# Gates, branches and the first half chunk of merge in one stage; exchanged banks and an earlier Gelu in the gather; unread products in pauses of TensorE

## The reference

```python
x = first_block(...)       # layer 0: retention; layer 1: forgetting attention; each h @ w_in, mixer, @ w_out
# second block
proj = rms_norm(x, mix_norm_w) @ w_in          # stick-breaking q k v, delta-rule q k v z b a, gate_sb, gate_gdn
o_sb  = stick_breaking_attention(q, k, v)
o_gdn = rms_norm(gated_delta_rule(...), gdn_out_norm_w) * silu(z)
merged = sigmoid(gate_sb) * (o_sb @ w_branch_sb) + sigmoid(gate_gdn) * (o_gdn @ w_branch_gdn)
x = x + merged @ w_out
h2 = rms_norm(x, ffn_norm_w)
# PEER: per token 8 heads x 16 experts out of 16384
s1, s2 = h2 @ w_q against keys1, keys2;  expert = top 16 of the sums of the top 16 of each
x = x + sum_e softmax(score)_e * gelu(h2 . u[e]) * v[e]
```

## Time and profile before

| | |
|---|---|
| median of 3 runs | 3151.41 us (3150.56 to 3151.66) |
| the profiled execution's own time | 3151.18 us |
| its span, first to last instruction | 3149.4 us |
| PE busy | 2786.7 us (88%) |
| DVE busy | 1850.0 us (59%) |
| ACT busy | 904.6 us (29%) |
| POOL busy | 738.3 us (23%) |
| mean granted TensorE clock | 0.954 |
| gather's queue (software_dynamic) | 536.90 MB, 41.0% of 16 engines' span |

### The profile page before, as it was taken

One profiled execution on the slowest core, in us unless ns is written; L12 is line 12 of the kernel. 1 busy time (PEld: TensorE's weight loads), 2 busy tenths in 40 slices (PEclk: granted clock), 3 DMA queues, 4 the chain that ended last, 5 costly groups with the idle time before them and its releaser, 6 DMA issues. The chain is left out here.

```text
span 3149.4 us, 29124 instructions
## 1 busy us (share of the span) xinstructions
PE 2786.7 (88%) x10720; PEld 1841.8 (58%) x10720; DVE 1850.0 (59%) x3613; ACT 904.6 (29%) x1686; POOL 738.3 (23%) x724
## 2 busy tenths in 40 slices
PE   7999999999899999999999989778777777777877
PEld 6887587766677677889877873333333333333333
DVE  7761634343543657455534478777677777777554
ACT  3123313433355746422422332111111111111111
POOL 0000210000110523253000124333333333333432
PEclk8999999999999999999999999998989989998999
DMA  7574655521545454644523379999999999999997
GB/s 277 206 275 164 184 180 169 187 81 54 174 160 187 134 189 161 220 132 125 200 80 127 107 269 420 422 421 422 422 422 422 422 422 422 422 422 422 422 422 309
DMA packets 190006, 840.75 MB, mean 267 GB/s; under 512 B 17060, under 2 KB 19364, under 8 KB 123431
## 3 DMA queue, kind: packets, MB, share of 16 engines
q0 software_dynamic: 73728, 536.90, 41.0%
q1 hardware_dynamic: 116136, 301.98, 28.1%
HBM read 828.34 MB, written 144.71 MB: 309 GB/s over the span
## 5 line engine op out<-in xcount | busy, mean ns | idle before, releaser
L230 DVE TENSOR_TENSOR weights_low<-weights_raw,weights_high 128x2048 fp32r<-128x2048 f32 x108 | 250.5, 2320 | 415.2 <-ACT weights_high L225 405.6
L225 ACT CAST weights_high<-weights_raw 128x2048 fp32r<-128x2048 f32 x108 | 206.0, 1907 | 612.8 <-PE proj_banks L288 594.5
L288 PE MATMUL proj_banks<-h_low,weights_high 128*128 128x512 f32 x896 | 357.3, 399 | 14.3 <-PEq L161 6.2
L288 PE MATMUL proj_banks<-h_high,weights_high 128*128 128x512 f32 x896 | 351.8, 393 | 0.0
L288 PE MATMUL proj_banks<-h_high,weights_low 128*128 128x512 f32 x896 | 351.8, 393 | 0.0
L3128 ACT ACTIVATE coef<-dots 128x4 f32<-128x4 f32 x126 | 25.9, 205 | 794.0 <-DVE dots L3006 794.0
L3109 ACT ACTIVATE sig<-shape_consts,coef 128x128 f32<-128x128 f32 x512 | 163.9, 390 | 251.1 <-DVE coef L3025 251.1
L288 PEld LDWEIGHTS proj_banks<-h_low,weights_high 128*128 128x128 f32 x896 | 170.1, 190 | 53.7 <-issue 17.3
L2906 PE MATMUL work_banks<-rows_over_split,sig 128*128 128x512 f32 x256 | 144.0, 703 | 54.6 <-ACT sig L3109 54.6
L288 PEld LDWEIGHTS proj_banks<-h_high,weights_low 128*128 128x128 f32 x896 | 170.1, 190 | 36.6 <-issue 1.9
L288 PEld LDWEIGHTS proj_banks<-h_high,weights_high 128*128 128x128 f32 x896 | 170.0, 190 | 36.0
(11 more groups left out here) (524 smaller groups left out, 5651.2 us busy)
## 6 DMA issues: line engine op xcount, KB each, us to landing
joined_rows<-in_peer_u_dram SPq DMA_DIRECT2D x64, 1024.0 KB, 7.2
joined_rows<-in_peer_v_dram SPq DMA_DIRECT2D x64, 1024.0 KB, 7.2
weights_raw<-in_w_in_dram SPq DMA_DIRECT2D x36, 1024.0 KB, 5.0
weights_raw<-in_ret_w_in_dram SPq DMA_DIRECT2D x24, 1024.0 KB, 5.3
ret_gate<-in_mod_w_dram SPq DMA_DIRECT2D x20, 1024.0 KB, 12.3
weights_raw<-in_fox_w_in_dram SPq DMA_DIRECT2D x16, 1024.0 KB, 5.4
weights_raw<-in_ret_w_out_dram SPq DMA_DIRECT2D x8, 1024.0 KB, 5.3
weights_raw<-in_peer_w_q_dram SPq DMA_DIRECT2D x8, 1024.0 KB, 5.4
```

The costliest lines, as they stand in the source:

```text
L225: nc.scalar.copy(whi[h][:, :, :], raw[h][:, :, :]).then_inc(high_ready[h], 1)
L230: nc.vector.tensor_tensor(wlo[h][:, :, :], raw[h][:, :, :], whi[h][:, :, :].bitcast(F32), ALU.subtract).then_inc(w_split[h], 1)
L288: last = nc.tensor.matmul(out_tile, lhs, rhs, start=(start and j == 0), stop=(stop and j == 2))
```

## The change

**The stage.** `gates` becomes `gated_branches`. Its block goes on after the four gate chunks with the two chunks of w_branch_sb, the two of w_branch_gdn and the first half of w_out's first chunk. The ends of three blocks become one. The inputs of the later products are split inside the earlier chunks: o_sb during gate chunks 1 and 2, the delta rule's output during the sb chunks, the merged tiles as each is added. They go into the places of tiles that are no longer used. `output_norm` gets the split input (`begun`) and starts at the second half of its first chunk. On ACT the second copy of each turned pair moves behind the sigmoids.

**The gather.** Rows and sums change banks: for even t they lie in `pb`, for odd t in `pa`. DVE waits for the last chunk's first two tiles only, ACT issues a Gelu on one column at once, then puts the first group's Gelu and diagonals between its four score copies. DVE waits for all score copies after the first group.

**The unread products.** `idle_products` issues fp32 products of the identity with constants into a bank that nobody reads after them. In program order there are 17: one ahead of each of the last three transpose groups of the retention's attention and two behind them, two at the end of each of the three `output_norm`, six at the end of the forgetting attention.

The diff, cut to its core:

```diff
@@ -337,6 +337,11 @@
+    def idle_products(to, n):
+
+        for _ in range(n):
+            nc.tensor.matmul(to, ident, cst[:, 0:S], start=True, stop=True)
+
@@ -388,7 +393,7 @@
-            inp = InputSplit(tag, src, input_parts(st, tag + "in_", tiles), tiles)
+            inp = begun or InputSplit(tag, src, input_parts(st, tag + "in_", tiles), tiles)
...
-                    load(sp, w_src, 1, g0 + 1)
+                    if begun is None:
+                        load(sp, w_src, 1, g0 + 1)
...
                     for c in range(n):
-                        half_product(c, 0, range(TT))
+                        if c or begun is None:
+                            half_product(c, 0, range(TT))
...
                     for t in range(TT):
                         turn(t)
+                    pe.wait_ge(tile_free[0], stored(1))
+                    idle_products(pb[:, 0, :], 2)
...
@@ -1087,7 +1100,9 @@
                         for n in range(RET_HEADS * TT - LAG, RET_HEADS * TT):
+                            idle_products(pb[:, 0, :], 1)
                             transposes(n)
+                        idle_products(pb[:, 0, :], 2)
@@ -1563,6 +1578,7 @@
                             values(m)
+                        idle_products(pb[:, 0, :], 6)
@@ -2566,11 +2582,16 @@
-    def gates(parts, qkv, sig, osb, ogt, o_away, z_away, then):
+    def gated_branches(parts, qkv, sig, osb, ogt, o_away, z_away, dead, kept):
...
+        SB, GDN, OUT = n, n + D // CW, n + 2 * D // CW
...
+        for tiles in dead:
+            tiles.close()
+        over_left, over_out, over_z = (sbuf(kept, "branch_in_over_" + k, [P, KT, S], F32R) for k in ("left", "out", "z"))
...
+            sb_in = InputSplit("sb_branch_", osb, (over_left, over_z), KT)
+            gdn_in = InputSplit("gdn_branch_", ogt, (over_out, over_osb), KT)
+            out_in = InputSplit("merge_", sig, (over_left, over_z), KT)
...
-                    for c in range(1, n):
-                        load(sp, columns(a["w_in_2"][0], 7 * D + 2 * H), c, g0 + c, join=False)
+                    for c in range(1, OUT + 2):
+                        load(sp, sources[min(c, OUT)], c, g0 + c, join=False)
...
                 @block.tensor
...
+                    for c in range(SB, OUT):
+                        inp = sb_in if c < GDN else gdn_in
+                        for h in range(2):
+                            project_half(pe, c, h, inp.parts, ready=inp.ready)
+                    project_half(pe, OUT, 0, out_in.parts, feature_major=False, ready=out_in.ready)
                 @block.vector
...
+                        if c == 1:
+                            sb_in.low(range(KH))
+                        elif c == 2:
+                            sb_in.low(range(KH, KT))
+                    dve.wait_ge(odd_read, TT)
+                    for c in range(SB, GDN):
+                        split_second(low, c)
+                        split_next(low, c)
+                        gdn_in.low(range((c - SB) * KH, (c - SB + 1) * KH))
+                        for t in range(4):
+                            m = 4 * (c - SB) + t
+                            dve.wait_ge(tile_full[t], g0 + c + 2)
+                            nc.vector.tensor_tensor(sig[:, m, :], sig[:, m, :], pb[:, t, :], ALU.mult
+                                                    ).then_inc(tile_free[t], 1)
+                    for c in range(GDN, OUT):
...
+                            if t:
+                                out_in.low(range(m - 1, m))
+                        out_in.low(range(4 * (c - GDN) + 3, 4 * (c - GDN) + 4))
+                    split_second(low, OUT)
                 @block.scalar
...
-                        for t in range(2 * c - 4, 2 * c - 2) if c >= 2 else ():
...
+                        if c >= 2:
+                            keep_odd(2 * c - 4)
                         for t in range(4):
                             act.wait_ge(tile_full[t], g0 + c + 2)
...
+                        if c >= 2:
+                            keep_odd(2 * c - 3)
+                        if c == 1:
+                            act.wait_ge(og_ready, TT)
+                            act.wait_ge(o_back, 16)
+                            sb_in.high(range(KH))
+                        elif c == 2:
+                            sb_in.high(range(KH, KT))
...
+                    for c in range(GDN, OUT):
+                        split_second(high, c)
+                        split_next(high, c)
+                        for m in range(4 * (c - GDN), 4 * (c - GDN) + 4):
+                            act.wait_ge(added, m + 1)
+                            out_in.high(range(m, m + 1))
+                    split_second(high, OUT)
-            stage_end(n)
+            stage_end(OUT)
...
@@ -2873,10 +2910,10 @@
-                return (pb[:, 0:2, :] if t % 2 else pa[:, 2:4, :]).rearrange("p b n -> p (b n)")
+                return (pa[:, 2:4, :] if t % 2 else pb[:, 0:2, :]).rearrange("p b n -> p (b n)")
...
-                return pb[:, 2 + half, :] if t % 2 else pa[:, half, :]
+                return pa[:, half, :] if t % 2 else pb[:, 2 + half, :]
@@ -2996,7 +3033,8 @@
-                    dve.wait_ge(sc_ready, 4 * n)
+                    for b in range(2):
+                        dve.wait_ge(tile_free[b], state["g"] + n + 1)
@@ -3049,6 +3087,8 @@
                                 weights_of(t, g)
+                                if g == 0:
+                                    dve.wait_ge(sc_ready, 4 * n)
@@ -3098,16 +3138,25 @@
+                    nc.scalar.activation(coef[:, 0, 0:1], eps[:, 0:1], ACT.Gelu).then_inc(gelu_table, 1)
...
+                    for t in range(TT):
+                        if t == TT - 2:
+                            act.wait_ge(dot_done, PRE + GE)
+                            act.wait_ge(gelu_table, 1)
+                            nc.scalar.activation(coef[:, 0, :], dots[:, 0, :], ACT.Gelu).then_inc(gelu_done, 1)
+                        act.wait_ge(s_full, 4 * (n - 1) + t + 1)
+                        if t == TT - 1:
+                            act.wait_ge(coef_ready, 1)
+                            diagonals(0)
+                        nc.scalar.copy(sc[:, t, 4 * n - 4:4 * n, :],
+                                       pa[:, t, :].rearrange("p (f c) -> p f c", c=P)).then_inc(sc_ready, 1)
```

115 lines of the change are left out of this document (49 added, 66 removed).

## The result

| | before | after |
|---|---|---|
| median | 3151.41 us (5 runs, 3150.56 to 3153.49) | 3122.00 us (5 runs, 3120.72 to 3123.78) |
| the profiled execution's own time | 3151.18 us | 3121.36 us |
| its span | 3149.4 us | 3119.5 us |
| PE busy | 2786.7 us (88%) | 2795.8 us (90%) |
| DVE busy | 1850.0 us (59%) | 1852.3 us (59%) |

The change saves 29.4 us; the ratio is 0.9907, with a 95% interval from 0.9896 to 0.9918. The forecast was 3123.6 in a range from 3119.0 to 3132.5.

What follows compares the result with a forecast made beforehand. The prediction took DMA to bound the gather and PE everything ahead of it. Its terms, 7.6 + 16.8 + 1.2 + 2.2 = 27.8 us, taken from 3151.18 with the median 0.23 higher, gave 3123.6 us, range 3119 to 3132.5.

Steps and rivals of the forecast that it cites:

- What bounds the kernel: Whole kernel: DMA bounds the gather at 422 GB/s, PE bounds ahead of it; each us PE saves there shortens the end.
- Unread products ahead of the merge: Retention's attention, first output_norm, forgetting attention, second output_norm: gains of 1.9, 1.7, 2.7 and 1.3, sum 7.6 us.
- These lie between the two. I take them as held: Pauses left at first output_norm and forgetting attention, some 1.6 and 1.7 us, between 1.27 and 2.39: no low clock assumed.
- the 0.4 at the second `output_norm`: Second output_norm: unread products end at 884.8, DVE at 884.47; this later end is taken off the 1.7 us gain.
- behind 2.39 and more the slow stretch comes: Reading of PE's pauses: slow records follow pauses of 2.39 us and more, at once or 1 to 1.5 us later.
- the clock falls all the same: Rival: unread products fill only part of each pause; two pauses failing gives 3128.0 (0.13), all five 3134.1 (0.07).
- The joined stage: Gates to w_out: four pauses go, worth 1.4, 7.1, 4.3 and 4.0 us, sum 16.8, if the splits fit beside PE.
- The thinnest cover: Joined stage: x and a weight split take 10.1 us against PE's half chunk of 10.9, leaving 0.8 us; no wait assumed.
- the term for ACT's copies: Inside the gates: PE's 1.27 us wait for the sigmoids goes with ACT's second copy behind them, worth 1.4 us.
- Merge to the gather's stage: Behind the merge: two unread products save the clock's 1.6 us less 0.4 of a later end, 1.2.
- The opening: Gather's opening: earlier rows and first PE product close the DMA hole from 1875 to 1895, worth 2.2 us (1.6 to 2.7).
- The other rivals: Joined stage waits, 3129.5 (0.12); PE bounds the gather, 3159 (0.03); the end doesn't follow PE, 3148 (0.03).

Runs made afterwards that it cites:

- e4: The kernel before with the 17 unread products alone, without joined stage or new gather: 3145.23 us, 6.8 below before.
- e2: The changed kernel with the gather's part undone (old banks, all four score copies ahead of the first Gelu): 3126.43 us.
- e1: The changed kernel without its 17 unread products: 3129.69 us, 22.3 below before.
- e10: The kernel of e7 with one unread product instead of two behind the retention's last transposes: 3118.35 us.
- e11: The changed kernel with twelve unread products instead of six at the end of the forgetting attention: 3124.73 us.
- e12: The kernel of e7 with only the two added unread products at the start of the two early output_norm, none between turned groups: 3118.35 us.
- e3: The kernel before with the joined stage alone, no unread products and the old gather: 3135.36 us, 16.6 below before.
- e6: The changed kernel with both of ACT's copies of turned pairs ahead of the four sigmoids again: 3126.14 us.
- e5: The changed kernel with exchanged banks, but all four score copies on ACT ahead of table load, first Gelu and first diagonals: 3122.71 us.
- e8: The changed kernel with the forgetting attention's split input placed 32 bytes further in SBUF: 3121.99 us.
- e9: The kernel of e7 with 4096 bytes between the high and low part of the forgetting attention's split input: 3118.84 us.
- e7: The changed kernel with five more unread products, two at the starts of the early output_norm and three between turned groups: 3118.81 us.

## Why the prediction was right

- **What bounds the kernel** held: 25.8 us were saved on PE up to the last score tiles, 4.1 from there to the end, 29.9 in all; the gather's middle is unchanged at 422 GB/s.
- **Unread products ahead of the merge** (7.6 in the sum): 5.65 in the profile; with the merge's 1.2 it is 6.8 in e4 against 8.8. The step that failed is "These lie between the two. I take them as held". Of the two pauses left between 1.27 and 2.39 us the first (1.67) held. The other, which I had at 1.9 at most, is 2.08, since its six products add 5.16 us to PE's work and not 5.4, and it did not hold in this execution, though it did in those of e2 and e4. It took back 1.7 of the 2.7. Behind it a second low stretch came at 871, where transposes and unread products themselves ran at half clock: at 816.95 the kernel after is 5.88 us ahead, at 881.85 only 4.43.
- Two things that I had not in the sum gave some back. The low stretch at 395 to 399 (1.7 us), which no pause of ours stands ahead of, is gone in the kernel after; it is missing in e1 too, without the products, so it can't be put down to them. And the retention's output starts 0.07 us later, not 0.9, since PE came to the first of its last three groups of transposes at 372.00 instead of 372.55, and its two products cost the other 0.6. Two small sums were off as well: ACT's last copy and PE's two products lie 378.05 - 377.05 = 1.0 apart by the earlier trace rows, not 0.9, and the 0.4 at the second `output_norm` is 884.8 - 884.47 = 0.3.
- The reading under it, "behind 2.39 and more the slow stretch comes", was wrong for the 2.39 itself: there the clock had fallen before the pause (e1). And the kernel before has a pause of 1.96 us among its turned groups, at 877.67, with no low clock behind it, which would have spoken for the two as held; e10 and e11 show how little such a single trace says.
- **The rival "the clock falls all the same"** was therefore half true: of its two failing pauses one fails in some executions, by all that the times show. What that costs, 3.6 us with the second stretch, is the difference between the median of 3122.0 and the 3118.4 of e12. The Trainium skill (TensorE: Matmul & The Clock Gate, Part 1: The HAM clock gate) says that the number of slow products at the start of one kernel varies from run to run. I had used that for the length of a stretch. The traces of e2, e4 and the kernel after differ in whether there is a stretch at all, in the middle of the kernel.
- **The joined stage** (16.8): 16.6 in e3 alone (17.3 in its trace, from the first product behind the second `output_norm` to the first w_q product), 18.55 in the profile of the whole, of which 1.4 is the product distance, 0.3 the cheaper block end (0.47 against the 0.80 of the earlier trace rows) and 0.4 that the low stretches cost 2.75, 1.72 and 1.7 instead of 2.6, 1.6 and 1.6. The thinnest cover, x ahead of a weight split, held: no pause stands in the output behind 1698.20. Within it the term for ACT's copies was undersized: 1.4 against the 2.8 of pauses in e6, where a second pause comes with the first.
- **Merge to the gather's stage** (1.6 of clock less 0.4): 1.62 in the profile, and in e1 the clock is low there without the products.
- **The opening** (2.2): 4.1 in the profile, 5.7 between e3 and e1, about 5 over all traces. The mechanism was right, the size was off: I took the earlier trace rows from 1875 on, while the rate had been down since 1868. With the window set from the first score product on, the trace of before would have given 4.0.
- **The other rivals** did not come: no pause in the joined stage, the gather's granted clock at 0.91 (before 0.92) is far above 0.72, and the end followed PE.

The two terms that were too small (opening and joined stage, 4.1 together) and the one too large (2.0 in the unread products) half cancelled: 3123.6 came closer to 3122.0 than its parts deserved.

## What to carry to other kernels

A pause of TensorE of 2.4 us or more was paid twice in this kernel, by its length and by the low clock in or behind it; products that nobody reads save the second part, as long as they end before the engine that the stage waits for, and the best place for one more is behind the block's end, where PE waits for the next input anyway (e12, 3118.35 us, the fastest kernel of this study together with e10). For a hole in a transfer queue, set the window from the last moment at which the queue was surely fed, not from where the hole looks deepest. And where a pause near a limit is left, one profile doesn't tell the clock of all executions: lay the times of several beside it.

## What the runs showed of the hardware

- At the stage ends ahead of the gather, no pause of 1.78 us or less had a low clock behind it in these profiles, and each of 2.39 us and more had. At the 2.39 us pause of the kernel before the clock had fallen already among the transposes ahead of it, with PE pausing for 1.46, 0.77 and 0.77 us between them, so 2.51 us is the shortest pause that shows the fall by itself.
- Between those lengths the traces differ. The 2.08 us pause has a low clock behind it in four (the kernel after, e5, e6, e8) and not in two (e2, e4); the 1.81 us pause in e10 and not in e9; the 1.96 us pause among the turned groups in five (those four and e11) and not in six (before, e1, e2, e3, e4, e12). With the pause of 2.08 us filled at its end (e7, e9, e10, e12) 15 of 16 executions lie from 3117.15 to 3119.71 us and one at 3121.42; the nine of the kernel after and of e8 lie from 3120.72 to 3123.78, and of the four of e5 three do about (3122.52 to 3124.27) and one is at 3116.35.
- With six unread products ahead of the forgetting attention's output, a low stretch there and one among the turned groups 50 us later came together in four traces (817 and 871 in the kernel after, in e5, e6 and e8), and neither in e2, e4 and e12; e11 has the second alone. In the kernel before, e1 and e3, with the 7.23 us pause, the first came without the second. That the one brings the other is not shown. Together they cost 3.6 us.
- The same fp32r products run at a distance of 0.2267 or 0.2343 us in two stages of the same shapes, and the merge's changed from the one to the other when its stationary operand came to lie in another place of SBUF. That the place is the cause is not shown: 32 bytes further gives 0.2323 (e8), 4096 bytes more between the parts 0.2343 (e9).
